# Two memory heads in one attention step, a negated score pass, and value sets spread anew, in a one-core decoder layer

## The chip, the cores and the metric

The kernel runs on one core of a Trainium2 chip. Five engines work side by side and meet through semaphores: TensorE (PE; its weight loads are shown as PEld), VectorE (DVE), ScalarE (ACT), GpSimd (POOL) and SyncE (SP), which only starts transfers here. Transfers of all queues share 16 DMA engines. The metric is the device time of one execution in microseconds (us), the median of several runs; lower is better.

## The reference

One layer of a hybrid decoder for 1024 prompt positions and 8 sample sequences, in float32. After a norm and one projection of 2308 columns, four head groups run side by side, each 256 wide (4 heads of 64):

- A, forgetting attention: `softmax(q k^T / 8 + c_q - c_k)`, causal. The prompt attends to itself; each sample attends to 4096 cached positions, which lie as 32 pages of 128 rows, found by a page table.
- B, spatial gating inside chunks of 128 positions.
- C, dilated attention with a relative bias, and M, attention to 256 memory tokens:

```
def mem_attend(q, mk, mv):
    sc = jnp.einsum('bthe,bmhe->bhtm', q, mk).astype(jnp.float32) * (1.0 / math.sqrt(e))
    p = jax.nn.softmax(sc, axis=-1)
    return jnp.einsum('bhtm,bmhe->bthe', p.astype(mv.dtype), mv)
```

The group outputs are normed, joined, projected and added; then a convolutional feed-forward part with 2816 hidden columns follows.

## The kernel before

The program has three parts: the projection (a list of `units`, one for each 128 rows and column block), the attention steps, and output projection with feed-forward part. Every float32 product is made from a high part and a remainder, which are split in `hi` (ScalarE copies) and `lo` (VectorE subtracts).

The change is in the attention steps and just before them. A step `g` is one head and one tile of 128 queries; there are 96 = 12 heads x 8 tiles. Heads come in the order of four of group A (steps 0 to 31), four of M (32 to 63), four of C (64 to 95). In A and C (`two(H)` is true) a tile sees 8, 7, ... 1 blocks of 128 keys; in M always 2. The step runs over five engines, each of which goes through the same loop over `g` in its own program order:

- TensorE: `tp(g-2)` transposes the weights of step g-2 (L931, L936), `prep` transposes the queries or keys of the next head in tiles 4 to 7 (L898, pieces q0, k0, q1, k1), `qk(g)` makes the scores (L921, L922), `v_sum(k)` adds one set of four cached value pages for the samples (L966), `pv_(g-3)` makes the product with the values (L947).
- VectorE: `evb` copies transposed blocks 5 to 8, `score(g)` adds the bias and takes the row maximum (L1786), negates it (L1791), or reduces it for M (L1794); `lo`; `out(g-3)` scales by the reciprocal of the sum (L1808, L1811). Behind these come sample tasks tied to steps: the 64 granules of cached keys (`k_dot`, L1536 and L1539; 48 of them between the projection's units, 16 in steps 0 to 15), ten dots with the cached keys of C and M (`cm_dot`, L1821 and L1823; steps 38 to 43, then from step 50), maxima and sums.
- ScalarE: `eva` copies blocks 1 to 4 (L1268), `hi`, `ex(g)` is the exponential (L1262), and in steps 0 to 11 half of the value pages' loads (L359).
- GpSimd: issues two value pages of every set (L359), all cached values of C and M (L385), the maxima over partitions (L2143) and the inverse roots of the norms (L2137, L2140).
- SyncE: in order of `g`, key pages (four of a set), two value pages of a set from set 12 on, then queries, keys and values of later heads, bias rows (toeA, toeC) and output weights.

Sets of keys (`ring`) and of values (`vring`) have four slots each: the load of set k waits until set k-4 is used. Which value sets belong to which step says `v_step`:

```
V0, V1, V2 = 12, 26, 34
v_step = [4 + k for k in range(V0)] + [16 + (k - V0) * 16 // (V1 - V0) for k in range(V0, V1)] + \
    [32 + (k - V1) * 32 // (V2 - V1) for k in range(V1, V2)] + [64 + (k - V2) * 23 // (NV - V2) for k in range(V2, NV)]
```

With 64 page sets and ten of C and M that is 12 sets in steps 4 to 15, 14 in 16 to 31, 8 in the memory steps, 40 in steps 64 to 86. Sum 66 needs a load that GpSimd issues behind the inverse root of three groups (its wait for 24 squares, `o_sq`).

Of the kernel before, what the change touches and what calls it, by code (L numbers as in the profile page):

```python
# [97 lines left out]
def build(nc, t):  # L98
# [5 lines left out]
    with ctx:  # L104
# [46 lines left out]
        q1c, o = at("q1c", [HD + 2, 2, SEQ], f32r, o); klc, o = at("klc", [HD + 2, 2, SEQ], f32r, o)  # L151
# [36 lines left out]
        nm, o2 = at("nm", [P, 2, 2], f32, o2)  # L188
        rc, o2 = at("rc", [P, 2], f32, o2)
# [201 lines left out]
        HEADS = [(ATT, hh) for hh in range(NH)] + [(MEMG, hh) for hh in range(NH)] + [(DIL, hh) for hh in range(NH)]  # L391
# [10 lines left out]
        def nblk(g):  # L402
            return NT - g % NT if two(g // NT) else 2
# [4 lines left out]
        for g_ in range(STEPS):  # L408
# [37 lines left out]
        CMK_AT = {38 + i: i for i in range(6)}  # L446
        CMK_AT.update({50 + i: 6 + i for i in range(4)})

# [4 lines left out]
        def _(sp):  # L453
# [51 lines left out]
            def qk_load(hp):  # L505

                grp, par = HEADS[2 * hp][0], hp % 2
# [42 lines left out]
            def v_load(hp):  # L550

                grp, par = HEADS[2 * hp][0], hp % 2
# [30 lines left out]
            for n in range(NKP, NKP + 3):  # L583
                k_load(n)
# [12 lines left out]
            for g in range(STEPS):  # L597
                H, s = divmod(g, NT)
                hp = H // 2
# [12 lines left out]
                if H >= 2 and H % 2 == 0 and s == 3 and hp + 1 < 6:  # L612
                    sp.wait_ge(S("s_pv"), 8 * H)
                    v_load(hp + 1)
# [4 lines left out]
                if 38 <= g < 45:  # L619
                    k_load(NKA + 3 + g - 38)  # L620
# [3 lines left out]
                if g == 47:  # L624
                    for hh in range(2):
                        toe_load(toeC[:, hh, :], 1 + hh, f"toeC_ld{hh}")
                if g == 48:
                    for d in range(2):
                        sp.dma_start(wost[d][:, :, :], t["w_outL"][DORD[d]]).then_inc(S(f"wo_ld{d}"), 16)
                if H in (9, 10) and s == 1:  # L630
                    sp.wait_ge(S("s_nm"), 8 * H)
                    toe_load(toeC[:, (H - 9) % 2, :], H - 6, f"toeC_ld{(H - 9) % 2}")
# [1635 lines left out]
```

## Time and profile before

| | us |
|---|---|
| median of 3 runs | 1603.72 |
| lowest and highest | 1597.79, 1605.02 |
| the profiled execution | 1595.72 |
| its span | 1594.1 |
| TensorE busy | 1455.5 |
| VectorE busy | 973.4 |
| ScalarE busy | 462.8 |
| GpSimd busy | 187.1 |
| mean granted clock of TensorE | 0.915 of full |

The profiled execution's own time is 8 us below the median. Busy time of TensorE counts pipelined matmuls, so a busy TensorE is not one at its peak, and the granted clock says at which of two levels, 1.2 or 2.4 GHz (0.5 and 1.0), it ran. Queue names end in q (SPq is SyncE's queue); "idle before <-X" names what a wait ended with, and "issue" is time in which the engine waited for nothing that the profile shows.

### The profile page before, as it was taken

To read this page: it belongs to the slowest core of one execution; us is meant where nothing else is said; L and a number is where in the kernel's file an instruction comes from. 1 tells how busy PE (TensorE), PEld (TensorE's weight loads), DVE (VectorE), ACT (ScalarE), POOL (GpSimd) and SP (SyncE) were. 2 spreads that over 40 slices of the span, in tenths; PEclk is the share of its full clock that TensorE was granted. 3 is DMA by queue.
4 is the path that set the end of the run, shared out by engine and by line. 5 is a ranking of instruction groups with operands and counts; after the bars stand their busy time and mean duration, and the time that the engine had idled before them with its cause. 6 is when DMAs were issued, how large, how long until landed. Compare 5 with 4: busy or idle time off the path is not lost.

```text
span 1594.1 us, 26012 instructions
## 1 busy us (share of the span) xinstructions
PE 1455.5 (91%) x8749; PEld 1318.3 (83%) x8749; DVE 973.4 (61%) x1531; ACT 462.8 (29%) x724; POOL 187.1 (12%) x244
## 2 busy tenths in 40 slices
PE   6988999677989977879989999999999999999997
PEld 3777887555666655769979999999999999999997
DVE  7667699878777543643566556464555646454653
ACT  6322111233545443532233222121222212122220
POOL 5530034312311233000000000000000000000000
PEclk9899999867985777979989999999999999999999
DMA  7266565587765486304101020110202011020202
GB/s 249 74 195 210 165 197 175 165 233 215 238 169 166 139 239 171 87 27 155 40 0 54 27 80 28 54 53 27 67 14 80 22 60 53 28 67 14 80 1 117
DMA packets 125259, 168.79 MB, mean 106 GB/s; under 512 B 22758, under 2 KB 99583, under 8 KB 124723
## 3 DMA queue, kind: packets, MB, share of 16 engines
q1 hardware_dynamic: 100704, 129.45, 26.5%
q0 software_dynamic: 7616, 22.03, 4.8%
q10 hardware_dynamic: 16810, 15.61, 3.3%
q8 instruction: 79, 1.29, 0.3%
q14 instruction: 50, 0.40, 0.1%
HBM read 153.09 MB, written 13.96 MB: 105 GB/s over the span
## 4 chain that ended last, share of the span: by engine, by line
PE 60%; DVE 12%; issue 8%; SPq 5%; DMA 4%; POOL 3%; ACT 2%; POOLq 0%; ACTq 0%; DVEq 0%
PE ps L1025 16%; PE ps L1027 15%; PE ps L1026 15%; PE ps L947 4%; SPq L358 2%; SPq L359 2%; DVE ring L1536 2%; POOL rsn L2140 2%; PE ps L966 1%; PE ps L846 1%; PE ps L847 1%; PE ps L848 1%; POOL rsn L2137 1%; DMA fst<-in_w_upL 1%; DVE ulo L1989 1%
## 5 line engine op out<-in xcount | busy, mean ns | idle before, releaser
L1025 PE MATMUL ps<-hhi,uhi 128*128 128x344 f32 x1056 | 341.8, 324 | 11.6 <-DVE hlo L2011 4.9
L1027 PE MATMUL ps<-hhi,ulo 128*128 128x344 f32 x1056 | 340.4, 322 | 7.5 <-issue 7.5
L1026 PE MATMUL ps<-hlo,uhi 128*128 128x344 f32 x1056 | 340.5, 322 | 0.0
L1025 PEld LDWEIGHTS ps<-hhi,uhi 128*128 128x128 f32 x1056 | 201.6, 191 | 21.6 <-issue 18.4
L1026 PEld LDWEIGHTS ps<-hlo,uhi 128*128 128x128 f32 x1056 | 201.7, 191 | 0.0
L1027 PEld LDWEIGHTS ps<-hhi,ulo 128*128 128x128 f32 x1056 | 201.5, 191 | 0.0
L1025 PE MATMUL ps<-ahi,dhi 128*128 128x344 f32 x528 | 169.8, 322 | 3.6 <-DVE dlo L2114 3.6
L2043 DVE TENSOR_TENSOR uu<-ps,rstd_bc 128x1032 f32<-128x1032 f32 x44 | 54.2, 1233 | 191.5 <-PE ps L1027 191.5
L1026 PE MATMUL ps<-alo,dhi 128*128 128x344 f32 x528 | 170.0, 322 | 0.0
L1027 PE MATMUL ps<-ahi,dlo 128*128 128x344 f32 x528 | 169.2, 321 | 0.0
L846 PE MATMUL ps<-whi,hhi 128*128 128x512 f32 (+1 forms) x376 | 146.6, 390 | 13.2 <-DVE wlo L1496 12.0
L947 PEld LDWEIGHTS ps<-vst,pts 128*128 128x128 f32 x704 | 106.8, 230 | 55.1 <-issue 34.0
L848 PE MATMUL ps<-whi,hlo 128*128 128x512 f32 (+1 forms) x376 | 144.0, 383 | 0.0
L847 PE MATMUL ps<-wlo,hhi 128*128 128x512 f32 (+1 forms) x376 | 143.6, 382 | 0.0
L947 PE MATMUL ps<-vst,pts 128*128 128x65 f32 x704 | 121.1, 323 | 15.0 <-DVE oN L1811 14.8
L2076 DVE TENSOR_TENSOR x<-ps,x 128x1032 f32<-128x1032 f32 x80 | 98.3, 1229 | 14.0 <-PE ps L1027 11.7
L1025 PEld LDWEIGHTS ps<-ahi,dhi 128*128 128x128 f32 x528 | 99.7, 189 | 5.5 <-DVE dlo L2114 3.9
L1027 PEld LDWEIGHTS ps<-ahi,dlo 128*128 128x128 f32 x528 | 99.8, 189 | 0.0
L1026 PEld LDWEIGHTS ps<-alo,dhi 128*128 128x128 f32 x528 | 99.7, 189 | 0.0
L846 PEld LDWEIGHTS ps<-whi,hhi 128*128 128x128 f32 x376 | 73.7, 196 | 31.0 <-DVE wlo L1496 15.8
L359 POOL DMA_DIRECT2D vring<-in_cache_a_v x128 | 68.9, 538 | 195.4 <-issue 171.8
L1536 DVE TENSOR_TENSOR ring<-ring,qb 128x1024 f32<-128x1024 f32 x64 | 78.0, 1218 | 14.7 <-DMA ring<-in_cache_a_k 14.0
(238 smaller groups left out, 2344.5 us busy)
## 6 DMA issues: line engine op xcount, KB each, us to landing
fst<-in_w_upL SPq DMA_DIRECT2D x44, 512.0 KB, 3.7
ring<-in_cache_a_k SPq DMA_DIRECT2D x168, 128.0 KB, 2.6
vring<-in_cache_a_v POOLq DMA_DIRECT2D x128, 128.0 KB, 3.0
vring<-in_cache_a_v SPq DMA_DIRECT2D x104, 128.0 KB, 2.8
ring<-in_cache_a_k ACTq DMA_DIRECT2D x88, 128.0 KB, 2.5
fst<-in_w_down SPq DMA_DIRECT2D x22, 512.0 KB, 3.7
wst<-in_w_in SPq DMA_DIRECT2D x32, 256.0 KB
x<-in_xT SPq DMA_DIRECT2D x16, 258.0 KB, 3.1
```

The costliest lines, as they stand in the source:

```text
L358: page = sp.value_load(ptab[0:1, bass.ds(seq * PAGES + (group * 4 + j), 1)], min_val=0, max_val=NPOOL - 1)
L359: sp.dma_start(dst[:, slot, j, :], pool[bass.ds(page, 1)].rearrange("o p c -> p (o c)"))\
L846: pe.matmul(out, lh, whi[:, sl, 0:w], start=(kc == 0), stop=False)
L847: pe.matmul(out, lh, wlo[:, sl, 0:w], start=False, stop=False)
L848: i = pe.matmul(out, ll, whi[:, sl, 0:w], start=False, stop=(kc == KC - 1))
L947: i = pe.matmul(ps[:, 6, 0:HD + 1], pts[:, g % 2, j, :], vst[:, hp % 2, j, H % 2, :], start=(j == 0), stop=(j == nb - 1))
L1025: pe.matmul(out, lhs_hi(kc), rhs_hi(kc)[:, cs], start=(n == 0), stop=False)
L1026: pe.matmul(out, lhs_hi(kc), rhs_lo(kc)[:, cs], start=False, stop=False)
L1027: i = pe.matmul(out, lhs_lo(kc), rhs_hi(kc)[:, cs], start=False, stop=(n == nk - 1))
L1536: dve.tensor_tensor(kv, kv, q.broadcast_to([P, 4, WG]), ALU.mult).then_inc(S("k_mul"), 1)
L2043: dve.tensor_tensor(c3(uu[:, :]), U3(k % 2), c3(rstd_bc[:, :]), ALU.mult).then_inc(S("f_free"), 1)
L2076: dve.tensor_tensor(c3(x2[:, d, :]), U3(d % 2), c3(x2[:, d, :]), ALU.add).then_inc(S("f_free"), 1)
```

## The change

Seven things are edited together. (1) The memory group has two passes of eight steps instead of four: a step handles two heads of a pair for one query tile, with scores of both side by side (2 x 256) in one bank, two exponentials, four transposed blocks and both value products; there are 80 steps. Each head's score, transpose and value instructions stay separate. (2) `score` of A and C multiplies by -1 and keeps the minimum; the exponential gets scale -1 and that minimum as its bias, and the negation (L1791) goes. (3) The first head's `lo` pieces q0 and k0 come before the last `finish_norm`, ScalarE loads the exponential's table before the last unit's wait, and its first eight value-page issues come between k0 and q1. (4) The 48 key granules between units leave out the last two units, and the key loads 48 to 50 are issued before the wait for the projection's end. (5) Value sets: 12, 14, 16 and 32 in the four parts. (6) The dots of C and M go to steps 24, 26, ... 34 and 38, 40, 42, 44. (7) q1c takes the second half of the pair's queries, so that the zeros that C's heads needed in klc go, and C's remainder product uses 64 rows.

```
@@ tables
-        HEADS = [(ATT, hh) for hh in range(NH)] + [(MEMG, hh) for hh in range(NH)] + [(DIL, hh) for hh in range(NH)]
+        HEADS = [(ATT, hh) for hh in range(NH)] + [(MEMG, 0), (MEMG, 2)] + [(DIL, hh) for hh in range(NH)]
+        PAIR = [0, 0, 1, 1, 2, 3, 4, 4, 5, 5]
-                k_room[u_] = (2.9, 1.2, 4.0, 2.9, 3.6)[b_]
+                k_room[u_] = (2.9, 1.2, 4.0, 2.9, 3.6)[b_] if u_ < UI[(4, 6)] else 0.0
-        V0, V1, V2 = 12, 26, 34
+        V0, V1, V2 = 12, 26, 42
+        M0, C0 = 4 * NT, 6 * NT
-            [32 + (k - V1) * 32 // (V2 - V1) for k in range(V1, V2)] + [64 + (k - V2) * 23 // (NV - V2) for k in range(V2, NV)]
+            [M0 + (k - V1) * 16 // (V2 - V1) for k in range(V1, V2)] + [C0 + (k - V2) * 23 // (NV - V2) for k in range(V2, NV)]
-        CMK_AT = {38 + i: i for i in range(6)}
-        CMK_AT.update({50 + i: 6 + i for i in range(4)})
+        CMK_AT = {24 + 2 * i + (2 if i >= 6 else 0): i for i in range(NCM)}
@@ SyncE
+            for n in range(NKP, NKP + 3):
+                k_load(n)
             sp.wait_ge(S("z_done"), NU)
...
-            for n in range(NKP, NKP + 3):
-                k_load(n)
             c_rows(1)
...
-                if H >= 3 and H % 2 == 1 and s == 0 and hp + 1 < 6:
-                    sp.wait_ge(S("p_tp"), PN[(H, "k1" if two(H) else "q1")])
-                    qk_load(hp + 1)
+                if s == 0 and H in (3, 4, 5, 7):
+                    sp.wait_ge(S("p_tp"), PN[(H, "k1" if two(H) else "q1")] if H != 4 else PN[(3, "k1")])
+                    qk_load({3: 2, 4: 3, 5: 4, 7: 5}[H])
-                if g == 46:
+                if g == 36:
                     sp.wait_ge(S("k_used"), NKA + 6)
                     sp.dma_start(qb[:, :, :], bass.AP(scr_qs.tensor, scr_qs[2].offset, [[0, P], [1, 8 * WG]])).then_inc(S("qb_ld"), 16)
@@ TensorE, qk
+                    q_ = qhl if s < 4 else q1c
+                    for a in range(2):
+                        q0, c = a * 512 + (s % 4) * P, a * NMEM
+                        out = ps[:, bank_, c:c + NMEM]
+                        pe.matmul(out, q_[:, p, q0:q0 + P], khh[:, p, c:c + NMEM], start=True, stop=False)
+                        i = pe.matmul(out, q_[0:HD, p, q0:q0 + P], klc[0:HD, p, c:c + NMEM], start=False, stop=True)
@@ TensorE, pv_
+                        a, m = divmod(j, 2)
+                        i = pe.matmul(ps[:, 6, a * (HD + 1):(a + 1) * (HD + 1)], pts[:, g % 2, j, :], vst[:, hp % 2, m, a, :],
+                                      start=(m == 0), stop=(m == 1))
@@ ScalarE
+            act.activation(fb[:, 0:1], fb[:, 0:1], ACT.Exp)
             act.wait_ge(S("z_done"), NU)
...
+                if two(g // NT):
+                    m = act.activation(lg[:, g % 2, 0:W], lg[:, g % 2, 0:W], ACT.Exp, scale=-1.0, bias=nm[:, g % 2, 0:1])
+                else:
+                    for a in range(2):
+                        c = slice(a * NMEM, (a + 1) * NMEM)
+                        m = act.activation(lg[:, g % 2, c], SBANK(g % 2)[:, c], ACT.Exp, bias=nm[:, g % 2, 1 + a:2 + a])
...
-            for s in PREP_AT:
-                hi(0, PREP_AT[s])
+            hi(0, "q0")
+            hi(0, "k0")
+            value_pages(0)
+            hi(0, "q1")
+            hi(0, "k1")
@@ VectorE
+            dve.wait_ge(S("z_done"), NU)
+            lo(0, "q0")
+            lo(0, "k0")
             finish_norm(pending)
-
-            dve.wait_ge(S("z_done"), NU)
+            lo(0, "q1")
+            lo(0, "k1")
...
-                    dve.tensor_tensor_reduce(out=lg[:, g % 2, 0:W], in0=SBANK(g % 2)[:, 0:W], in1=bias_, scale=1.0,
-                                             scalar=-3.0e38, op0=ALU.add, op1=ALU.max, accum_out=nm[:, g % 2, 0:1])\
-                        .then_inc(S("s_lg"), 1)
-                    lgs[0] += 1
-                    T_.wait("s_lg", lgs[0])
-                    dve.tensor_scalar(nm[:, g % 2, 1:2], nm[:, g % 2, 0:1], -1.0, None, ALU.mult).then_inc(S("s_nm"), 1)
+                    dve.tensor_tensor_reduce(out=lg[:, g % 2, 0:W], in0=SBANK(g % 2)[:, 0:W], in1=bias_, scale=-1.0,
+                                             scalar=3.0e38, op0=ALU.add, op1=ALU.min, accum_out=nm[:, g % 2, 0:1])\
+                        .then_inc(S("s_nm"), 1)
...
-                if g in (33, 34):
-                    T_.wait("s_qk", 8 * (g - 30))
-                    dve.memset(klc[HD:HD + 2, g - 33, :].bitcast(f32), 0.0).then_inc(S("c_zero"), 1)
```

The other sample tasks keep their order and move with the steps (small batch 45 to 36, maxima 55 to 45, the weights' scaling 68 to 56), the squares of the memory group from steps 72 to 79 to steps 56 to 63, and GpSimd's two maxima waits from sets 33 and 36 to sets 35 and 43.

## Rows read from the trace of the kernel before

**Rows 1.** The page: its span, and TensorE's granted clock in 40 equal slices.
```profile
span 1594.1 us, 26012 instructions
...
PEclk9899999867985777979989999999999999999999
```

**Rows 2.** Stretches: length, busy (times) of each engine, granted clock, DMA share, GB/s.
```profile
200.00:300.00 100.00, 98.10 (x432) 79.20 (x430) 91.82 (x132) 17.60 (x33) 36.57 (x32) 1.00 0.63 187
...
320.00:335.00 15.00, 8.48 (x35) 7.83 (x36) 11.22 (x21) 4.43 (x7) 1.32 (x3) 0.50 1.06 284
...
429.00:449.80 20.80, 20.73 (x189) 15.87 (x187) 13.28 (x44) 11.89 (x21) 7.51 (x14) 1.00 0.69 205
449.80:466.00 16.20, 12.91 (x98) 9.64 (x95) 12.63 (x32) 8.13 (x20) 2.68 (x5) 1.00 0.41 115
...
485.00:512.00 27.00, 24.42 (x101) 18.46 (x101) 20.07 (x43) 13.15 (x42) 3.67 (x7) 0.50 0.59 184
...
540.20:612.50 72.30, 62.91 (x509) 45.59 (x505) 34.79 (x101) 33.14 (x67) 29.38 (x54) 0.85 0.76 220
```

**Rows 3.** Timeline of ScalarE: start, us, engine, line, instruction, idle before it.
```profile
301.29 0.59 ACT L1247 ACTIVATE qhl<-ps 64x512 fp32r<-64x512 f32 x1
...
314.46 1.28 ACT L1262 ACT_TABLE_LOAD   x1
319.06 1.15 ACT L1262 ACTIVATE lg<-lg,nm 128x1024 f32<-128x1024 f32 x1 [3.32 <-DVE nm L1791]
319.74 8.31 ACTq L359 DMA_DIRECT2D vring<-in_cache_a_v  x8
328.09 1.04 ACT L1262 ACTIVATE lg<-lg,nm 128x896 f32<-128x896 f32 x1 [7.89 <-DVE nm L1791]
...
401.62 1.15 ACT L1262 ACTIVATE lg<-lg,nm 128x1024 f32<-128x1024 f32 x1 [4.79 <-DVE nm L1791]
...
449.85 0.47 ACT L1262 ACTIVATE lg<-ps,nm 128x256 f32<-128x256 f32 x1 [0.51 <-DVE nm L1794]
```

**Rows 4.** Timelines of SyncE's queue and of VectorE: key sets and a granule.
```profile
308.96 12.82 SPq L359 DMA_DIRECT2D ring<-in_cache_a_k  x12
...
337.02 12.67 SPq L359 DMA_DIRECT2D ring<-in_cache_a_k  x12
...
342.57 1.23 DVE L1536 TENSOR_TENSOR ring<-ring,qb 128x1024 f32<-128x1024 f32 x1 [5.97 <-DMA ring<-in_cache_a_k]
```

**Rows 5.** Timeline of TensorE at full clock, memory step.
```profile
462.36 0.66 PE L947 MATMUL ps<-vst,pts 128*128 128x65 f32 x4 [0.52 <-DVE oN L1811]
...
463.60 0.61 PE L966 MATMUL ps<-vring,sA 128*4 128x256 f32 x8
```

**Rows 6.** Chain that ended last, memory steps at half clock: start, us, what.
```profile
489.77 0.96 PE ps L966 x8
...
492.94 1.04 PE ps L947 x4
493.98 0.43 PE ps L931 x2
...
495.13 1.06 PE ps L947 x4
```

**Rows 7.** Timeline of VectorE: a negation, a dot's first instruction, a memory score.
```profile
428.61 0.15 DVE L1791 TENSOR_SCALAR nm<-nm 128x1 f32<-128x1 f32 x1
...
462.21 1.22 DVE L1821 TENSOR_TENSOR ring<-ring,qb 128x1024 f32<-128x1024 f32 x1
...
464.60 0.41 DVE L1794 TENSOR_REDUCE nm<-ps 128x1 f32<-128x256 f32 x1
```

**Rows 8.** Timeline of GpSimd: a page issue and the inverse root.
```profile
610.38 0.54 POOL L359 DMA_DIRECT2D vring<-in_cache_a_v  x1 [0.62 <-issue]
...
621.10 0.20 POOL L2137 TENSOR_SCALAR rso<-sso 128x24 f32<-128x24 f32 x1 [8.71 <-issue]
621.39 4.22 POOL L2140 TENSOR_TENSOR rso<-rso,nhalf 128x24 f32<-128x24 f32 x1
```

More of the change, by code:

```diff
@@ L402, in nblk @@
         def nblk(g):
-            return NT - g % NT if two(g // NT) else 2
+            return NT - g % NT if two(g // NT) else 4
         def qtile(g):
@@ L1260, in ex @@
                     T_.wait("s_tpa", g - 1)
-                src = lg[:, g % 2, 0:W] if two(g // NT) else SBANK(g % 2)[:, 0:W]
-                act.activation(lg[:, g % 2, 0:W], src, ACT.Exp, bias=nm[:, g % 2, 1:2]).then_inc(S("s_exp"), 1)
+                if two(g // NT):
+                    m = act.activation(lg[:, g % 2, 0:W], lg[:, g % 2, 0:W], ACT.Exp, scale=-1.0, bias=nm[:, g % 2, 0:1])
+                else:
+                    for a in range(2):
+                        c = slice(a * NMEM, (a + 1) * NMEM)
+                        m = act.activation(lg[:, g % 2, c], SBANK(g % 2)[:, c], ACT.Exp, bias=nm[:, g % 2, 1 + a:2 + a])
+                m.then_inc(S("s_exp"), 1)
             def eva(g):
@@ L1299, in o_square, with value_pages @@
                 sq_no[0] += 1
-            for s in PREP_AT:
-                hi(0, PREP_AT[s])
+            def value_pages(g):
+                for n in V_PAIR.get(g, ()):
+                    if n < V0:
+                        if n >= 4:
+                            T_.wait("v_used", n - 3)
+                        load_pages(act, vpool, n // 8, n % 8, n % 4, (2, 3), vring, "vs_ld")
+            hi(0, "q0")
[3 more added lines that the diff above has]
+            hi(0, "k1")
             for g in range(STEPS + 4):
@@ L1312, in _ @@
                     ex(g)
[L1313 to L1317 removed]
+                if g > 0:
+                    value_pages(g)
                 if g == 2:
@@ L1321, in _ @@
                     samp_exp(1)
-                if g == 62:
+                if g == 51:
                     samp_exp_cm()
@@ L1743, in _, with lo @@
                     early_softmax()
+            def lo(H, piece):
+                T_.wait("p_hi", PN[(H, piece)])
+                i, p = int(piece[1]), H % 2
+                if not two(H):
+                    for a in range(2):
+                        r0 = a * HD
+                        if piece[0] == "q":
+                            q_, c = q1c if i else qhl, slice(a * 512, (a + 1) * 512)
+                            m = dve.tensor_tensor(q_[HD:P, p, c], ps[r0:r0 + HD, 1, 0:512], q_[0:HD, p, c].bitcast(f32), ALU.subtract)
+                        else:
+                            c = slice(a * NMEM, (a + 1) * NMEM)
+                            m = dve.tensor_tensor(klc[0:HD, p, c], ps[r0:r0 + HD, 3, 0:NMEM], khh[0:HD, p, c].bitcast(f32),
+                                                  ALU.subtract)
+                    m.then_inc(S("p_lo"), 1)
+                    return
+                c, r0 = slice(i * 512, i * 512 + 512), p * HD
+                if piece[0] == "q":
+                    m = dve.tensor_tensor(qhl[HD:P, p, c], ps[r0:r0 + HD, 4 if H == 0 else 1, 0:512], qhl[0:HD, p, c].bitcast(f32),
+                                          ALU.subtract)
+                else:
+                    m = dve.tensor_tensor(klc[0:HD, p, c], ps[r0:r0 + HD, 5 if H == 0 else 3, 0:512], khh[0:HD, p, c].bitcast(f32),
+                                          ALU.subtract)
+                m.then_inc(S("p_lo"), 1)
+            dve.wait_ge(S("z_done"), NU)
+            lo(0, "q0")
+            lo(0, "k0")
             finish_norm(pending)
-            dve.wait_ge(S("z_done"), NU)
+            lo(0, "q1")
+            lo(0, "k1")
             dve.memset(vst[:, :, :, :, HD:HD + 1].rearrange("p a t h e -> p (a t h) e"), 1.0).then_inc(S("dve_set"), 1)
```

160 lines of the change are left out of this document (79 added, 81 removed).

## The prediction

> **What bounds the kernel now.** The page comes first [rows 1]: of 1594.1 us the middle slices are where TensorE's clock and its busy digits break; from about 690 us on the feed-forward part runs at nearly full clock and the change does not touch it. So the change has to be read between 299 and 683 us. The second view is the table of stretches [rows 2]; the third is ScalarE's timeline, where the exponential (L1262) of a step marks it: step 0 begins at 319.06, step 16 at 401.62 and step 32, the first memory step, at 449.85 [rows 3]; step 64, the first dilated one, at 540.2, where a stretch of rows 2 begins. The reader is to see four limits in a row, not one:
>
> - Steps 0 to 15: the queue of SyncE. It issues twelve key-page loads in 12.82 us, so 1.07 us a page and 4.3 us a set of four, and VectorE stands 5.97 us waiting for such a page at 342.57 [rows 4]. A step takes (401.6 - 319.1)/16 = 5.2 us [rows 3].
> - Steps 16 to 31: TensorE, busy 20.73 of 20.80 us in the last eight, at full clock [rows 2].
> - Steps 32 to 63: 90.4 us, 2.8 us a step, for little work. First at full clock; then dots of 1.22 us, two instructions for each of ten (L1821, L1823), make VectorE set the pace (2.45 for the dot, 0.41 for the score, two small instructions that I estimate at 0.4: about 3.2 us a step), the clock goes down, and it stays at half even when TensorE is again the bound: busy 24.42 of 27.00 us at 0.50 [rows 2, 5 to 7].
> - Steps 64 to 80: GpSimd's queue. It needs 0.54 + 0.62 = 1.16 us for a value page and has two of each set, 2.31 us a set, and it issued some 27 sets in these 72.3 us [rows 2, 8]. Then its reciprocal root: 8.71 us of nothing and 4.22 us of work with the next value loads queued behind [rows 8].
>
> **The change, part by part.** The sum is made against the profiled execution, 1595.72 us (span 1594.1), which lies 8.0 below the median of 1603.72.
>
> *Projection.* The 48 key granules lose the last two units, so the others take 7% more. VectorE is 91.82 busy of 100 there, TensorE 98.10 [rows 2]; an estimated 60 of VectorE's 92 us are granules (two instructions of 1.22 us each, like the dots of rows 7), and 7% of them is 4 us more, 96 of 100: it still fits beside TensorE's own work, which hides it. I take +1, bounds 0 and +3.
>
> *Start of attention.* Now VectorE splits the first head only after its last granules. After the change the first two pieces go ahead. But ScalarE puts its eight value-page issues between k0 and q1: 8.31 us [rows 3]. Its four copies of 0.59 us begin at 301.29 today [rows 3]. They would begin at about 302.8, since the table load of 1.28 us, which today hides in a wait of 3.32 us, and an exponential of one column now lie ahead of them; k0 would end at 305.2, the issues at 313.5, q1 and k1 at 315.9 against 314.46, where the table load begins today [rows 3]. Step 0 thus comes 1.5 to 2 us later, the first bias row's load too, since 12.82 us of key loads are put ahead of it on SyncE's queue [rows 4]. In return, step 1's exponential no longer stands 7.89 us behind these issues and that score [rows 3], the data rush of 284 GB/s between 320 and 335 (share 1.06) is spread [rows 2], and the key loads of granules 48 to 50, today issued from 308.96, go from about 299.5 (before the last unit's end). Granule 51's load, today issued at 337.02 behind them and all the small ones [rows 4], moves with them, to about 328: 9 us earlier. The Trainium skill ("ScalarE: Activation LUTs", What ACT_TABLE_LOAD costs) adds a drain of about 1.4 us to the load; by it step 0 would be another 1.4 later. The row shows 1.28 and the next wait swallows whatever follows, so no run here shows it.
> What is late next is TensorE, which ran at 0.50 there [rows 2]: scaled from the two-block step of rows 6 (2.19 us), an eight-block one is near 7 us. So I count only 6 us won by step 16; bounds 0 and -10.
>
> *Steps 24 to 31.* Four of the ten dots land here: 4 x 2.45 = 9.8 us of VectorE, plus 1.8 for the second half of the pair's splits (three more subtractions, estimated at 0.4 to 0.7 from the reduction of 256 elements), less 1.2 for negations. VectorE: 13.28 + 9.8 + 1.8 - 1.2 = 23.7 us, in 20.8 [rows 2, 7]. At least +3; all four dots in the open +9.8. VectorE must finish them before the next score, and steps 28 and 30 are narrow for TensorE, so I take +6.
>
> *Memory steps, sixteen instead of 32.* TensorE's work per head and tile stays: value products, transposes and scores take 463.60 - 462.36 = 1.24 us at full clock, and 495.13 - 492.94 = 2.19 us at half; a value set 0.61 or 0.96 [rows 5, 6]. So a double step costs 2 x 1.24 + 0.61 = 3.1 us at full clock and 2 x 2.19 + 0.96 = 5.3 at half. Added are 26 transposes for the next heads (0.43/2 = 0.21 us each at half [rows 6], half that at full). VectorE: a double score (0.41 us for 256 elements, 1.22 for 1024 [rows 7]: about 0.68), some 0.5 to scale, six dots = 14.7, ten splits at 0.4 to 0.7, one batch of small work at 4: some 44 us in all, less than TensorE in either case, and with two slots a dot waits behind TensorE, not ahead of it. Stage at full clock: 16 x 3.1 + 3 + some 5 of stalls (the batch at step 36, the query load of 1 MB at 36 that step 38 needs) = 58 us. At half: 85 + 5.5 + 4 = 95 us. Against 90.4. Between these lies the clock alone. Before, it was full through 449.8:466 with TensorE busy 12.91 of 16.20, fell in the run of dot steps, and was 0.50 all through 485:512 [rows 2]. Now the dots are spaced by two steps, and each step carries twice the work and a value set. I take two thirds of the stage at full clock: 70 us, -20; bounds -32 and +5.
> The Trainium skill ("TensorE: Matmul & The Clock Gate", Part 1) says that sustained activity releases the throttle; by it this stage, with TensorE hardly idle, is at full clock, 58 us, and the total 12 us lower. The trace of before speaks against it: busy 24.42 of 27.00 and still 0.50 [rows 2].
>
> *Dilated steps to the root.* Sixteen value sets instead of eight are summed in the memory steps, so 32 instead of 40 are left. GpSimd's 18 page sets after step 48 take 42 us instead of 27 sets in 62 to 70; it stops being the bound. TensorE takes over: 48.2 us for the sixteen steps 16 to 31 with 14 sums [rows 3], plus 9 more sums of 0.6 = 53.6, and 2.4 for w_out and lost clock: 56 against 72.3, -16. The stretch's 220 GB/s moved 15.9 MB [rows 2]; nine sets of 0.52 MB less is 11.2 MB, 51 us at that rate, so DMA does not bind. Bounds -24 (no stall at all) and -8 (sets still arriving late).
> *From the root on.* GpSimd's 8.71 + 4.22 us remain [rows 8], now started by the squares of step 63; sums 66 on wait as before and nine steps follow the last sum, as before: 0, bounds 0 and +4.
>
> *Negation.* The 0.15 us of L1791 and its wait go from all 64 wide steps [rows 7]; exponential starts 0.2 us earlier. TensorE or a queue covers nearly all: -3; bounds 0 and -13. I find no ground for min or the scale of -1 to cost another time: operand count and width are the same. The two memsets go, in VectorE's slack: 0.
>
> Sum: +1 - 6 + 6 - 20 - 16 - 3 = -38 us. 1595.72 - 38 = 1557.7, and on the median 1603.72 - 38 = 1566.
>
> **Rivals.**
> 1. *Full clock through the memory steps*: 58 us there, -50 in all, 1554. For it: TensorE denser than in 449.8:466. Against: narrow matmuls did not bring the clock back before [rows 2].
> 2. *Half clock through them*: 95 us, and the same eight-sum relief afterwards, so -38 + 25 = -13, 1591. For it: the four dots in steps 24 to 31 open gaps in TensorE in the narrow steps 28 to 31, so the stage may begin at 0.50 and stay there.
> 3. *Slower than before*: the value sets. Sixteen sets in sixteen steps need SyncE for two pages each (2.2 us), with its own query, key and value-head loads in between. If one in-order SyncE load that waits (the query row at step 36 waits for six dots, the next pair's load for transposes) holds value pages, TensorE stands at the sum, the clock falls, and stage and start give back all. It decides from 38 us, which is 2.4 us lost in each memory step on top of the mix; half clock (+25) and 13 more, 0.8 a step: 1604 and above. Against it: a load has three steps of lead, some 11 us, against the 5.55 us from the first issue of such a page set to the use that rows 4 show (337.02 to 342.57).
> 4. *The dilated stage does not gain* (landing time, not the queue, set its 2.9 us a sum): -38 + 12 = -26, 1578.
>
> **How the numbers follow.** Chances: forecast with its mixed clock (1558 to 1574) 0.35; rival 1 (1542 to 1558) 0.20; rival 4 0.18; rival 2 0.19; rival 3 0.05; a start or a dilated stage better still 0.03. One run of this kernel against another differs by up to 0.45% (1597.79 to 1605.02), so within 0.5%, 8 us, is no change. The range runs from 1543 (rival 1 with the better bounds of start and dilated stage, in part) to 1597 (rival 2 with steps 24 to 31 in the open). Faster by over 0.5% (under 1595.7): all of 1 and 4 and the forecast, six tenths of rival 2, 0.87; within: the rest of rival 2, 0.08; slower: 0.05.
>
> **What would show it.** Memory steps between 58 and 75 us with the granted clock over 0.75 in them; the last value page issue by GpSimd not in a solid run of 1.16 us; step 0 at about 321 and step 16 at about 396; steps 24 to 31 taking 27 us with TensorE waiting for scores. Wrong it is if the clock of the memory stage is 0.5 throughout, if TensorE waits there for DMA, or if SyncE's queue reaches key set 51 no earlier than 335.

## The result, and the profile after

The changed kernel takes 1540.67 us (median of 4 executions, 1530.17 to 1574.85), the kernel before 1600.76 (4 executions, 1596.35 to 1605.02). The ratio is 0.9603, 95% interval 0.9522 to 0.9684; it leaves out executions over 1.5% above a kernel's own fastest, the medians do not. In a second comparison it is 0.9606 (0.9576 to 0.9637), with 1544.87 us (6 executions, 1533.39 to 1590.97) against 1604.31. The forecast was 1566 in a range of 1543 to 1597: the direction was right, the size was not, and the time lies 2.3 us below the range.

The profiled execution took 1533.76 us. The page's span and granted clock in 40 slices, as in [rows 1]:

```profile
span 1532.1 us, 25795 instructions
...
PEclk9899998967899999789999999999999999999999
```

The table of stretches, columns as in [rows 2]. The first line is the last 60 us of the first of [rows 2], the fourth (memory steps) to 449.80:466.00 and 485.00:512.00, the fifth to 540.20:612.50:

```profile
240.00:300.00 60.00, 51.55 (x211) 41.03 (x211) 55.34 (x72) 9.12 (x19) 24.79 (x21) 0.91 0.58 176
300.00:335.00 35.00, 18.28 (x74) 13.73 (x72) 13.52 (x28) 8.41 (x16) 10.68 (x16) 0.71 0.61 183
335.17:406.20 71.03, 58.68 (x390) 44.34 (x391) 63.39 (x110) 29.33 (x50) 12.96 (x25) 0.76 0.73 215
458.92:511.62 52.70, 51.69 (x404) 35.51 (x403) 39.95 (x81) 32.50 (x82) 18.12 (x34) 1.00 0.95 295
511.62:576.50 64.88, 59.60 (x494) 41.46 (x493) 34.88 (x93) 36.69 (x87) 23.93 (x40) 0.97 0.67 202
576.50:632.00 55.50, 47.69 (x359) 35.05 (x357) 32.93 (x97) 26.20 (x48) 7.37 (x9) 0.94 0.40 112
```

Cut at the exponentials of the same steps, the two spans differ by 62.0 us in this way (us, granted clock in brackets; steps of before, with those of after behind them):

| stretch | before | after | difference | predicted |
|---|---|---|---|---|
| up to step 0 | 319.1 | 335.2 | +16.1 | |
| steps 0 to 15 | 82.6 (0.69) | 71.0 (0.76) | -11.6 | +1 - 6 for both |
| steps 16 to 23 | 27.2 (0.94) | 27.6 (0.86) | +0.4 | 0 |
| steps 24 to 31 | 21.1 (1.00) | 25.2 (1.00) | +4.1 | +6 |
| memory steps 32 to 63 (32 to 47) | 90.4 (0.59) | 52.7 (1.00) | -37.7 | -20 |
| dilated, first 16 steps | 74.0 (0.85) | 64.9 (0.97) | -9.1 | -16 |
| dilated, last 15 steps | 66.6 (0.82) | 55.5 (0.94) | -11.1 | 0 |
| the rest | 913.3 (0.97) | 900.1 (0.98) | -13.2 | 0 |

The forecast's last term, -3 for the negation, has no line of its own. The reader is to see that three of the eight lines lie far below the forecast, by 42 us together: the memory steps at full clock throughout, and two stretches for which nothing had been forecast, the second of them code that the change does not touch. The start up to step 16, the first dilated steps and the negation gave some 19 us less than forecast. The total is therefore nearer to the forecast than its terms are, and that is luck.

**The start.** TensorE's waits in 240:335, by line, with the sum, the number and the longest:

```profile
PE ps L922 <- DMA klc<-scr_c: 10.8, 1, 10.8
PE ps L847 <- DVE wlo L1531: 8.1, 1, 8.1
```

SyncE's queue, then ScalarE and VectorE, as in [rows 3, 4]:

```profile
310.04 0.34 SPq L501 DMA_DIRECT2D o_vc<-zo  x1
...
311.71 12.78 SPq L359 DMA_DIRECT2D ring<-in_cache_a_k  x12
324.59 0.30 SPq L569 DMA_DIRECT2D klc<-scr_c  x1
...
326.08 3.06 SPq L565 DMA_DIRECT2D toeA<-scr_r  x1
...
341.45 0.38 SPq L359 DMA_DIRECT2D ring<-in_cache_a_k  x1
```

```profile
312.48 1.28 ACT L1249 ACT_TABLE_LOAD   x1
...
316.85 5.61 ACTq L359 DMA_DIRECT2D vring<-in_cache_a_v  x6
322.51 0.59 ACT L1271 ACTIVATE qhl<-ps 64x512 fp32r<-64x512 f32 x1 [6.35 <-issue]
...
335.17 1.15 ACT L1285 ACTIVATE lg<-lg,nm 128x1024 f32<-128x1024 f32 x1 [10.37 <-DVE nm L1835]
```

```profile
333.90 1.23 DVE L1835 CUSTOM_DVE_ANT_0 lg<-ps,toeA 128x1024 f32<-128x1024 f32 x1 [7.81 <-DMA toeA<-scr_r]
```

Two things delay step 0. With the key granules of the last two units spread over the others, more of them stand ahead of a weight split (L1531) in VectorE's queue: TensorE waits 8.1 us for that split, and in 240:300 it is busy 51.55 us at 0.91, where it was 58.10 at 1.00. VectorE's own busy time in these 60 us is no longer than before (55.34 against 55.88); what changed is the order in which things come. And the key loads go out not at 299.5 but at 311.71, since SyncE's queue first holds the outputs of the last unit but one (310.04). The forget rows (klc) and the bias (toeA) stand behind these 12.78 us, and the first score waits 7.81 us for toeA. Key set 51, which was to be issued at about 328, is issued at 341.45 (337.02 before).

### The profile page after: what moved, and what is told of

Its sections match the earlier page's. It is cut to its first block, busy times and chain, and to the rows that moved or that the text cites. A ratio compares the mean times of both kernels' runs of the same rounds, so it can differ in the third digit from the quotient of the medians.

```text
span 1532.1 us, 25795 instructions
## 1 busy us (share of the span) xinstructions
PE 1415.7 (92%) x8729; PEld 1281.2 (84%) x8729; DVE 953.0 (62%) x1417; ACT 457.6 (30%) x709; POOL 186.0 (12%) x244
## 3 DMA queue, kind: packets, MB, share of 16 engines
q8 instruction: 78, 1.28, 0.3%
## 4 chain that ended last, share of the span: by engine, by line
PE 65%; DVE 8%; SPq 7%; issue 6%; DMA 3%; POOL 2%; ACT 2%; ACTq 0%; DVEq 0%; POOLq 0%
PE ps L1037 17%; PE ps L1038 17%; PE ps L1039 17%; PE ps L955 3%; SPq L358 3%; SPq L359 2%; PE ps L978 2%; DVE ring L1571 1%; PE ps L938 1%; PE ps L847 1%; POOL rsn L2188 1%; PE ps L848 1%; PE ps L849 1%; PE ps L923 1%; DMA ring<-in_cache_a_k 1%
## 5 line engine op out<-in xcount | busy, mean ns | idle before, releaser
L955 PEld LDWEIGHTS ps<-vst,pts 128*128 128x128 f32 x576 | 74.9, 204 | 33.4 <-issue 24.0
L955 PE MATMUL ps<-vst,pts 128*128 128x65 f32 x576 | 84.0, 294 | 6.4 <-DVE oN L1858 6.3
L1428 ACT ACTIVATE convG<-uu,prm_a 128x1024 f32<-128x1024 f32 x22 | 27.5, 1248 | 201.7 <-DVE uu L2091 201.7
```

The costliest lines, as they stand in the source:

```text
L955: i = pe.matmul(ps[:, 6, 0:HD + 1], pts[:, g % 2, j, :], vst[:, hp % 2, j, H % 2, :], start=(j == 0), stop=(j == nb - 1))
```

## The experiments

All experiments start from the changed kernel unless said otherwise. "Start" is the exponential of step 0.

**The start's two edits, one at a time and both.** First the granules:

```
-                k_room[u_] = (2.9, 1.2, 4.0, 2.9, 3.6)[b_] if u_ < UI[(4, 6)] else 0.0
+                k_room[u_] = (2.9, 1.2, 4.0, 2.9, 3.6)[b_]
```

> The changed kernel, with the 48 key granules over all units again. Theory: the denser granules made VectorE the bound of the projection (TensorE waits 8.1 us once for VectorE's weight split, and part of the rest runs at half clock), and this alone is the 11 us by which the projection ended later (311.5 against 300.3). Then the projection ends at about 300 to 302, with TensorE waiting under 3 us for the split, while the gap from its end to step 0's exponential stays near 24 us or grows a little, since VectorE again has granules behind the last unit. Rival: the split was late by chance (a data transfer), and the projection's end stays at 306 to 312.

Then the key loads of granules 48 to 50 behind the bias, as before:

```
-            for n in range(NKP, NKP + 3):
-                k_load(n)
             sp.wait_ge(S("z_done"), NU)
...
             toe_load(toeA[:, :], 0, "toeA_ld")
+            for n in range(NKP, NKP + 3):
+                k_load(n)
```

> The changed kernel, with the key loads 48 to 50 behind the first bias row's load again. Theory: the twelve page loads (12.8 us of SyncE's queue) hold the first head's forget rows and bias row, for which TensorE waits 10.8 us and VectorE 7.8 us; with them behind, step 0's exponential comes about 18 us after the projection's end instead of 23.7, and the projection's end stays at 311. Steps 0 to 15 then take some 3 to 5 us longer than 71, because the key sets come later again. Rival: ScalarE's eight value-page issues between k0 and q1 (5.6 us) hold step 0; then the gap stays above 21 us.

And both together:

> Both of these undone together. Theory: projection ends at 300 to 302, step 0 at about 319 to 321, 14 us earlier than in the changed kernel; steps 0 to 15 take 72 to 78 us; the total is 8 to 14 us below the changed kernel, about 1520 to 1530 with steps of the same clock. Rival: the gain at the start is given back by key and value sets that come no earlier, and the total is within 4 us of the changed kernel.

Measured: start 329.4, 327.6 and 316.9 against 335.2; steps 0 to 15 then take 71.2, 74.1 and 81.8 against 71.0. So step 16 comes at 400.6, 401.7 and 398.7, against 406.2 in the changed kernel and 401.6 before. Undoing the granules alone brings 5.7 us (TensorE's wait for the split is 1.9 us then instead of 8.1), undoing the key loads alone 7.6, and undoing both 18.3, more than the sum of the two; but the first sixteen steps return 10.8 of it. Times: 1537.21 and 1545.3 (one execution each), and for both 1546.74 (6 executions, 1535.17 to 1574.11), ratio 0.9646 (0.9609 to 0.9683): no gain over the changed kernel can be told, where 8 to 14 us were expected.

Next, the value pages issued after the first exponential, as before (`value_pages(g)` also for g = 0):

> The changed kernel, with ScalarE's first eight value-page issues behind step 0's exponential again, as before. Theory: step 0 itself does not move (it waits for the bias row from SyncE's queue, 333.9), but step 1's exponential comes 6 to 8 us after step 0's instead of 3.4. If instead these issues were what made step 0 late, step 0 comes 5 us earlier.

Start 334.0, and step 1's exponential 9.2 us behind step 0's instead of 3.4. Steps 0 to 15 take 74.4, so that step 16 comes at 408.3, 2.2 us later than in the changed kernel and 1.2 later than in that kernel's second profile further down: in one execution, the early issue is worth a microsecond or two. The time was 1578.78 us; the memory steps ran at half clock here (90.7 us).

**What the clock does in the memory steps.** The experiment with both start edits back was at half clock there. Its stretch of the same sixteen steps, columns as in [rows 2]:

```profile
451.27:541.98 90.71, 90.71 (x403) 61.73 (x403) 40.64 (x81) 34.73 (x82) 18.07 (x34) 0.50 0.57 172
```

The same matmuls take 52.7 us at 2.4 GHz and 90.7 at 1.2 GHz, where TensorE has no idle time at all. At half clock, then, the sixteen double steps take as long as the 32 single ones did (90.4): all that is won there hangs on the clock. The Trainium skill ("TensorE: Matmul & The Clock Gate", Part 1) says that sustained activity releases the throttle; this row does not agree: busy 90.71 of 90.71 us and 0.50. The changed kernel itself was profiled once more, unchanged, beside the padded kernels further down:

> The changed kernel itself again, for how its executions spread. Two states theory: the times fall into groups near 1530 to 1535 and near 1570 to 1578, with some between, and each execution's mean granted clock goes with its time (0.95 or more when fast, 0.925 or less when slow). Rival: one group with a spread of 1%, the first measurement's 1574.9 being a disturbance.

1544.87 us, and 64.6 us in the memory steps of the profiled execution (1544.71 us). The six times lie at 1533, 1544 to 1545 (three) and 1585 to 1591. Over all ten executions of this kernel the mean granted clock goes with the time: 0.950 to 0.956 for the three under 1535, 0.942 to 0.944 for the four from 1544 to 1548, 0.909 to 0.925 for the three above 1570. Steps 30, 32, 36 and 38 of that execution, two steps a line:

```profile
453.99:459.65 5.66, 4.55 (x33) 2.95 (x32) 5.35 (x11) 1.66 (x6) 1.07 (x2) 0.87 0.83 256
459.65:468.33 8.68, 8.68 (x39) 5.31 (x39) 4.54 (x8) 2.55 (x6) 2.14 (x4) 0.50 0.74 194
...
478.82:490.55 11.73, 11.73 (x61) 8.79 (x57) 6.33 (x20) 5.84 (x14) 2.60 (x5) 0.57 0.67 209
490.55:496.72 6.17, 6.17 (x51) 4.27 (x50) 5.85 (x10) 2.67 (x7) 2.14 (x4) 1.00 0.45 136
```

And steps 30 and 32 of the first execution:

```profile
453.25:458.92 5.67, 4.49 (x37) 3.33 (x37) 5.35 (x11) 1.67 (x6) 1.08 (x2) 1.00 0.86 257
458.92:463.96 5.04, 5.01 (x38) 2.98 (x37) 4.38 (x8) 2.21 (x6) 2.15 (x4) 1.00 0.58 136
```

Program and work are the same; in both, TensorE waits 0.3 us in step 29 and 1.1 us in step 30 for VectorE's scaled output (1.4 us in all, cut at the exponentials). The clock falls at the end of step 30 in the one and not in the other. Having fallen it stays at half up to step 37; in other kernels of these experiments up to 43, 45, 49 or 51. That is 24 to 113 us of half clock in which TensorE was never idle.

**Does that idle time tip it?** The kept profiles can be counted. Nine kernels or executions with the double steps have that 1.1 us in step 30: in six the clock falls there (the second profile of the changed kernel, granules, both start edits, late value pages, value sets as before, 57 waits), in three it does not (the first profile, key loads behind, scores twice). Three more kernels change the idle time. One shortens it:

```
-        CMK_AT = {24 + 2 * i + (2 if i >= 6 else 0): i for i in range(NCM)}
+        CMK_AT = {g_: i for i, g_ in enumerate((22, 24, 26, 28, 32, 34, 38, 40, 42, 44))}
...
+                if g == 30:
+                    out(g - 3)
                 if piece and (piece != "k1" or two(H + 1)):
                     lo(H + 1, piece)
-                if g >= 3:
+                if g >= 3 and g != 30:
                     out(g - 3)
```

> Two edits to the changed kernel, both aimed at the one place where TensorE stands idle before the memory steps: in steps 30 and 31 it waits 0.30 and 1.11 us for VectorE's scaled outputs, which stand behind the splits of the next pair and a dot. Here the output goes ahead of the split in step 30, and the first four dots stand at steps 22, 24, 26 and 28 instead of 24 to 30. In the nine profiles so far of kernels with the double steps, this idle time was the same 1.4 us in 5.66, and afterwards the granted clock stayed at 1.00 in some (memory part 51 to 53 us) and fell to 0.50 in the others (65 to 91 us). Theory: this idle stretch is what tips the clock. Then the memory part takes 50 to 54 us at 1.00 here, the runs lie together (1525 to 1545) and the median is 1532, some 10 us under the changed kernel's. Rival: the clock falls for a reason that has nothing to do with this place (the chip's own phase or what came before step 28). Then the spread stays: median 1540 to 1547, one run in three above 1570.

A second adds the granule edit above to it:

> The same two edits and the key granules of the last two projection units put back as well, which took 5.7 us off the start and 3 to 6 us off the time up to step 16 in the single look at that edit alone. If the idle stretch tips the clock, the median is 1528 (1520 to 1540) and this is the fastest version; if it doesn't, 1537 with runs up to 1580.

A third makes the idle time longer:

```
+                if g == 30:
+                    cm_dot(CMK_AT[g])
                 if g >= 3:
                     out(g - 3)
...
-                if g in CMK_AT:
+                if g in CMK_AT and g != 30:
                     cm_dot(CMK_AT[g])
```

> The opposite edit to the changed kernel: in step 30 the dot (two instructions, 2.45 us) is put ahead of the output, so that TensorE waits 2.4 us longer there, 3.5 us instead of 1.1 in one piece. If this idle stretch tips the clock, it falls every time: the memory part takes 65 us or more in the profile at a clock of 0.50 to 0.8, and every run is at 1555 or above, median 1575. If the clock falls for another reason, the runs lie like those of the changed kernel plus at most 2.4 us: lowest about 1535, median 1543 to 1549.

Steps 30 and 31 of the first, then of the third of these kernels, and steps 32 and 33 of the third:

```profile
455.12:459.68 4.56, 4.39 (x35) 3.07 (x34) 3.18 (x9) 1.66 (x5) 1.05 (x2) 1.00 0.65 231
```

```profile
453.93:463.19 9.26, 5.64 (x32) 3.88 (x31) 5.63 (x11) 1.77 (x5) 1.07 (x2) 0.77 0.52 159
463.19:472.19 9.00, 9.00 (x43) 5.50 (x39) 4.54 (x8) 2.55 (x6) 2.15 (x4) 0.50 0.69 197
```

The shortened one: idle 4.56 - 4.39 = 0.17 us instead of 1.18 in the two steps, memory steps 52.9 us at 1.00 in the profile (52.7 at 1.00 with the granules), yet its six executions are 1532, 1534, 1537, 1563, 1566 and 1589 us, median 1549.95. The spread that was to go is still there. With the granules: 1546.61 (1531.45 to 1566.88), ratio 0.9588 (0.9558 to 0.9619), not to be told from the changed kernel's 0.9606. The lengthened one: memory steps 65.3 us at 0.77, and none of its four executions is under 1548 (1548.37, 1549.80, 1568.10, 1584.62; median 1558.95), where the changed kernel, in ten, has three under 1535. Its clock fell in the profile as forecast, but two executions are under the 1555 that was to be the least, and the median came 16 us lower than forecast. Of its excess, 3.6 us are the longer steps 24 to 31 themselves (28.8 against 25.2). So in the profiles the clock fell there in none of two with 0.2 us of idle time, in six of nine with 1.1, and in the one with 3.6; but taking the idle time away does not bring the slow executions to an end. The profiles show other occasions: with the key loads behind, the memory steps ran at 1.00 and the last fifteen dilated ones at 0.74 (63.5 us instead of 55.5); with the dots in runs, further down, the clock fell in step 38. What tips the clock in the slower executions of the shortened kernel was not profiled and stays open.

**Work added in the same steps.** Each high score product of the memory steps is done twice (32 more matmuls; the first result is overwritten):

```
+                        pe.matmul(out, q_[:, p, q0:q0 + P], khh[:, p, c:c + NMEM], start=True, stop=True)
                         pe.matmul(out, q_[:, p, q0:q0 + P], khh[:, p, c:c + NMEM], start=True, stop=False)
```

> The changed kernel, in whose memory steps the first score matmul of each head is done twice (the same result is overwritten), 32 more matmuls of 256 columns. Two states theory: the changed kernel's memory part takes 52.7 us at full clock in some executions and 90.7 at half in others, since single executions spread over 40 us. If more work per step makes the full clock surer, the part takes 60 to 63 us in the profile and the spread over executions shrinks to under 20 us, with a median near 1545. If the extra work does nothing for the clock, the spread stays at 40 us and the times are 8 to 15 us above the changed kernel's, at both ends.

Memory steps 54.8 us at 1.00, 2.1 more than the 52.7, not the 60 to 63 expected. The executions spread over 46 us, so the added work did not make the full clock surer. The time is 1561.53 us (1550.43 to 1596.43), ratio 0.975 (0.9712 to 0.9787), but 17 us of the difference to the changed kernel lie in the rest (917.4 against 900.1), which the next experiments explain.

**The parts of the change alone.** The kernel before with only the dots and their loads moved (at 24, 26, ... instead of 38 to 43 and 50 to 53):

> The kernel before, with only the ten dots moved to where the change has them (steps 24, 26 to 34, 38 to 44), single-head memory steps kept. If the runs of dots were what put the clock down, the memory part (32 single steps) falls from 90 us to 60 to 68 us with the granted clock over 0.85, and most of the change's 38 us there comes from the dots' places, not from the double steps. If the double steps did it (work per step dense enough), the clock stays near 0.5 to 0.6 here and the part takes 80 to 92 us.

1604.85 us (10 executions), ratio 1.0029 (1.0002 to 1.0055): nothing is won by that alone. The memory steps take 92.8 us at 0.58; TensorE still waits there, up to 4.1 us in one step, and the clock falls in step 33 and again in step 38. The other way, the changed kernel with its dots in two runs (33 to 38 and 41 to 44):

> The changed kernel, with the dots in two runs, in memory steps 33 to 38 and 41 to 44 (small batch at step 40). Dots' places theory: VectorE sets the pace there (about 2.45 + 1.4 = 3.9 us a step), the clock falls as it did before, and the memory part takes 75 to 90 us instead of 52.7. Double-step theory: a step has enough work on TensorE to keep the clock, and the part takes 56 to 64 us.

1566.84 us in one execution. Memory steps 65.6 us (0.82), then 71.3 (0.86) and 74.7 (0.59) against 64.9 and 55.5: the lower clock reaches far past the dots. TensorE waits 1.0, 1.2 and 1.3 us in steps 36 to 38 here, and the clock falls in step 38. But the changed kernel's own second profile has 64.6 us in the memory steps too. Since the clock varies from execution to execution, one execution can't say how much of the 33 us is the dots' own. What it does settle is the price of the dots in steps 24 to 31: with none there these steps take 22.8 us, against 25.2 with four, and the kernel before goes from 21.1 to 23.7 when they are moved in. So 2.4 to 2.7 us of the 4.1 are theirs.

The kernel before with only the negation taken out (score pass with scale -1 and minimum, exponential with scale -1):

> The kernel before, with only the negated score pass (minimum kept, no separate negation). Theory: 64 small instructions and their waits go, but a queue or TensorE covers nearly all of them: 0 to 5 us faster. Rival: it lies on every step's path, 0.2 us each, and is worth 13 us.

1601.65 us (10 executions), ratio 1.0014 (0.9989 to 1.0039): no effect that can be told.

The changed kernel with the value sets spread as before:

```
-        V0, V1, V2 = 12, 26, 42
+        V0, V1, V2 = 12, 26, 34
```

> The changed kernel, with eight value sets in the memory steps and 40 in the dilated ones, as before. Theory of the prediction: the dilated steps are bound by GpSimd's two page issues of 2.31 us for a set again, so steps 48 to 63 take 72 to 76 us instead of 65; the memory part loses eight sums of 0.6 us, 48 instead of 52.7. In all 3 to 8 us slower. Rival: without the sums the memory steps' TensorE work is thin enough for the clock to fall, and that part gets longer (over 60 us).

1596.9 us. It was at half clock in the memory steps, so it is compared with the experiment above that was at half clock too. Its three stretches (memory, dilated first 16, last 15), and behind them the two dilated ones of that experiment:

```profile
458.17:541.54 83.37, 83.37 (x343) 61.07 (x339) 40.58 (x81) 34.40 (x82) 9.46 (x18) 0.50 0.45 136
541.54:622.51 80.97, 74.94 (x535) 50.40 (x527) 34.89 (x93) 36.97 (x87) 29.48 (x54) 0.81 0.70 203
622.51:695.31 72.80, 62.18 (x388) 44.11 (x388) 33.60 (x97) 26.99 (x49) 10.43 (x10) 0.76 0.35 98
```

```profile
541.98:612.63 70.65, 64.97 (x503) 45.15 (x495) 34.87 (x93) 36.83 (x88) 24.04 (x40) 0.90 0.63 185
612.63:667.58 54.95, 48.11 (x359) 35.26 (x357) 32.93 (x97) 26.14 (x48) 7.18 (x9) 0.94 0.40 113
```

Eight sums fewer save 90.71 - 83.37 = 7.3 us in the memory steps, and the dilated ones take 10.3 and 17.9 us more: net 20.9 us. Most of these 28.2 us is not the sums' own. TensorE's idle time grows by 4.1 us only (6.03 + 10.62 against 5.68 + 6.84), eight sums are 4.9 us at full clock and 7.7 at half [rows 5, 6], and the rest is clock: half up to step 51 instead of 49, and 0.76 instead of 0.94 in the last fifteen steps. Two kernels that keep the new sets had low clocks in these fifteen as well (63.5 us at 0.74, 74.7 at 0.59). So in one execution each it isn't shown that the old spread costs 20.9 us.

What can be told is the idle time of the last fifteen steps. It is 15.2 us before and 7.8 after, 12.8 to 15.9 in the three other profiles of variants of the kernel before, and 2.3 to 7.7 in the eleven others with double steps and new sets. In them the sets that stood behind GpSimd's root arrive late, before (first line) more than after:

```profile
629.72 1.04 PE L966 MATMUL ps<-vring,sC 96*4 96x256 f32 x8 [6.05 <-DMA vring<-in_cache_c_v]
```

```profile
582.28 1.03 PE L978 MATMUL ps<-vring,sC 96*4 96x256 f32 x8 [4.21 <-DMA vring<-in_cache_c_v]
```

The next sum waits 1.94 us before (632.69) and 1.37 after (584.69). In all, the sums of these steps wait 12.5 us before, for loads and for ScalarE's copy of a finished sum (mkd), and 5.6 after. With the old spread in the changed kernel they wait 9.1, with the new one in the experiment beside it 4.6, one execution each: that part, some 5 to 7 us, goes with the spread. No experiment takes the double steps alone, without the new value sets and the spaced dots.

**Code that the change does not touch.** The rest (output projection and feed-forward) fell by 13.2 us. TensorE in the first products of a pass of the feed-forward's loop, before and after:

```profile
1000.57 0.32 PE L1026 MATMUL ps<-hlo,uhi 128*128 128x344 f32 x1
1002.78 0.45 PE L1027 MATMUL ps<-hhi,ulo 128*128 128x344 f32 x1 [1.90 <-issue]
1003.03 0.49 PE L1025 MATMUL ps<-hhi,uhi 128*128 128x344 f32 x1
```

```profile
951.57 0.32 PE L1038 MATMUL ps<-hlo,uhi 128*128 128x344 f32 x1
951.72 0.32 PE L1039 MATMUL ps<-hhi,ulo 128*128 128x344 f32 x1
951.88 0.32 PE L1037 MATMUL ps<-hhi,uhi 128*128 128x344 f32 x1
```

Before, in each of the four passes (1002.78, 1143.30, 1282.38, 1423.00) TensorE stands 1.7 to 2.0 us for nothing that the trace shows, always at the sixth matmul of the pass, and the clock is 0.59 in the 3.2 us that follow. After, there is no such stop, and a pass takes 137.3 us instead of 139.4 to 140.4. The loop's code is the same; what the change altered is how many TensorE instructions stand ahead of it. The Trainium skill ("Runtime: NRT & Kernel Launch", Instruction fetch mechanics) says that instructions come in blocks of 256 and that a taken branch out of the blocks at hand stalls. Two kernels test it, with waits put on TensorE ahead of step 0, for its own count of finished units, which is full by then. In the changed kernel:

```
+            for _ in range(114):
+                pe.wait_ge(S("z_done"), NU)
```

The page counts 57 instructions more (25852 against 25795). In the kernel before there are 398 waits, and the page counts 199 more (26211 against 26012).

> The changed kernel, with 57 instructions of nothing but satisfied waits put into TensorE's stream before the attention steps, which brings the start of the feed-forward loop to where it lies in the kernel before, by a count of TensorE's instructions. Theory: the 13 us that the unchanged last part (from the last exponential to the end) gained, 913 to 900 us, come from where the loop's code lies: before, TensorE stands about 1.9 us in each of four passes, seven matmuls into the loop, waiting for nothing that the profile shows, and the clock falls behind it. Then the last part takes 911 to 916 us here, with four such gaps. Rival: the gap comes from data or clock phase, and the last part stays at 898 to 902.

> The kernel before, with 199 instructions of satisfied waits in the same place, which shifts the loop to where the changed kernel has it, 256 instructions further on. If the place of the loop's code modulo 256 instructions or less decides, the last part takes 898 to 902 us instead of 913, without the four gaps. If the period is another, it stays at 911 to 916.

The changed kernel with 57, then the kernel before with 199:

```profile
989.36 0.32 PE L1040 MATMUL ps<-hlo,uhi 128*128 128x344 f32 x1
991.38 0.45 PE L1041 MATMUL ps<-hhi,ulo 128*128 128x344 f32 x1 [1.70 <-issue]
```

```profile
1008.52 0.32 PE L1028 MATMUL ps<-hlo,uhi 128*128 128x344 f32 x1
1008.68 0.32 PE L1029 MATMUL ps<-hhi,ulo 128*128 128x344 f32 x1
1008.83 0.32 PE L1027 MATMUL ps<-hhi,uhi 128*128 128x344 f32 x1
```

Both came as forecast. The rest takes 915.4 us with the 57 (four stops of 1.70 to 2.25 us; the time, 1586.03, is also that of memory steps at 0.55) and 898.2 with the 199 (no stop, time 1590.84 against 1604.31). Each is one execution, but the rest does not vary as the memory steps do: it is 897.9 to 900.2 us in all eleven profiles with the loop where the change has it, and 913.3 to 916.6 in the three with the loop where it was before. The scores done twice, with 32 more matmuls, has the stops as well (1.89 to 3.20 us, the rest 917.4). That the place of the loop decides is shown in both directions; that the stop is the fetching of instructions fits what the Trainium skill says there, but no row names it.

The 199 waits also held back step 0 of the kernel before to 335.5, and steps 0 to 15 then took 73.3 us instead of 82.6. A late start gives back some nine us by itself, so most of the 11.6 us that steps 0 to 15 gain in the table comes with the late start alone. The changed kernel with both start edits back, which starts at 316.9, needs 81.8 us for them.

## Why the prediction was right and wrong

- **Projection, +1.** Wrong. VectorE at 96 of 100 was held to fit beside TensorE's work; the average (it measured 90.36 in 200:300, less than before) hid that the weight splits that TensorE needs stand in the same queue. TensorE waited 8.1 us, its mean clock in 240:300 fell to 0.91, and putting the granules back brings the start 5.7 us forward.
- **Start, -6 by step 16.** Wrong: with the projection +4.5. SyncE's three key sets were dated to 299.5 "before the last unit's end", but two units' outputs stand ahead of them in the queue (311.71), and what stands behind them, forget rows and bias, is what step 0 needs. The forecast named the bias behind these loads and let step 0 come only 1.5 to 2 us later; it came 16.1 later. One of the prediction's own signs of being wrong came true, key set 51 no earlier than 335 (341.45). Nothing was lost behind the table load: it ends at 312.48 + 1.28 = 313.76, and the next activation starts at 313.78.
- **Steps 24 to 31, +6.** +4.1; VectorE's dots hold TensorE as described, for 2.4 to 2.7 us of it.
- **Memory steps, -20.** The two bounds were right within 6 us (58 and 95 forecast, 52.7 and 90.7 measured). The mixture was not a fixed one of two thirds: executions lie at either end or between. The profiled one is rival 1, with -37.7; the kernel's second profile, at 1544.71 us and nearer to the median, has 64.6 us and -25.8. Why the clock held in some executions and fell in others stays open.
- **Dilated steps to the root, -16.** -9.1, at the weak end of the bounds. TensorE was busy 59.6 us, where 53.6 had been added up, and it waited 3.7 us for a late set and 1.6 for ScalarE's copy, as rival 4 had it in part.
- **From the root on, 0 (bounds 0 and +4).** The step that failed: a path of some 980 us was put at 0, its attention steps because the sums would wait as before, and the rest because the change doesn't touch it. It measured -11.1 for the last fifteen steps and -13.2 for the rest, and the bounds left no room for a gain. The first was to be had from the prediction's own reasoning: eight sums moved forward bring the whole queue forward, the root's hole included, and TensorE idles 7.8 us behind it instead of 15.2 (clock 0.94 instead of 0.82). The second was not in the change's text at all; but the four stops were in the trace of before, and if they had stayed, the 1540.67 would be 13 us more, near 1554, inside the range.
- **Negation, -3.** No effect within 0.4%, which leaves room for the 3 us forecast but not for the 13 of its bound.
- **Rivals 2 and 3.** The half clock happens, as rival 2 says, and costs 38 us there; its 1591 is the highest single execution (1590.97) by chance, since 38 us on top of the profiled 1533.76 are only 1572. Rival 3 did not happen: no sum waits for a load in the memory steps of the profile, where TensorE is idle 1.0 us of 52.7.

## What to carry to other kernels

Price a stretch that moves work forward up to its very end, not only up to the next unchanged block; and ask of each queue not when its engine is free but what stands ahead and behind in it. Where one kernel's executions spread by 4%, look at the granted clock of each stretch before comparing single profiles: here 38 us of one stage hang on it. When unchanged code in a loop gets faster or slower, look for stops without a releaser at the same instruction of each pass; shifting the loop by some instructions is a test and a remedy.

## What the runs showed that was not expected

- TensorE busy 90.71 of 90.71 us with a granted clock of 0.50, and the same work in 52.7 us at 1.00. The return to full clock came in step 37, 43, 45, 49 or 51, after 24 to 113 us in which TensorE had been busy all along.
- A stop of 1.7 to 3.2 us at the same matmul of each loop pass, brought by 57 and taken away by 199 instructions ahead of the loop, worth 13 to 17 us of 900 with the lower clock behind it.
- Fulfilled waits are not free on TensorE: with 199 of them TensorE stood 20.7 us ahead of its first score and step 0 came 16.4 us later in the kernel before, though 57 did not delay the changed kernel, where TensorE was waiting for a load anyway (start 333.6).
